# Expert rows picked straight from x, the norm's factor moved into the pick matrix, x in a place of its own, and tile 0 routed before tile 1

## The reference, cut to what matters

```python
h = rms_norm(x, norm_mix[l])
...
x = x + merged @ w_out[l]
h2 = rms_norm(x, norm_ffn[l])
x = x + hier_moe(h2, w_router_group[l], b_router_group[l], w_router_expert[l], b_router_expert[l],
                 w_expert_gate[l], w_expert_up[l], w_expert_down[l])
```

## Time and profile before

| | |
|---|---|
| time, median of 3 runs | 701.91 us (701.51 to 702.41) |
| the profiled execution's own time | 701.26 us |
| its span, first to last instruction | 699.1 us |
| PE busy | 615.8 us, 88% |
| DVE busy | 279.8 us, 40% |
| ACT busy | 199.6 us, 29% |
| bytes moved | 247.53 MB, mean 354 GB/s |

### The profile page before, as it was taken

The page is one execution under the profiler, slowest core; times in us unless marked ns, Lnnn a source line. Parts: engine busy times, 40 slices in busy tenths (PEclk is TensorE's granted clock), DMA queues, the critical chain, the costliest instruction groups (busy, mean ns, idle before and its releaser), DMA issues.

```text
span 699.1 us, 11551 instructions
## 1 busy us (share of the span) xinstructions
PE 615.8 (88%) x4690; PEld 373.8 (53%) x4690; DVE 279.8 (40%) x623; ACT 199.6 (29%) x334; POOL 28.5 (4%) x54
## 2 busy tenths in 40 slices
PE   8999999999999998999987788775878857797876
PEld 5887899999999893333332233322323323332333
DVE  6476976985474945333231112211112211120311
ACT  5684455473535433121111111111111111110111
POOL 2612000000000020000000000000000000000000
PEclk9999999999999999999997989999889998887999
DMA  9995347436479799999999999999999999999995
GB/s 314 309 373 185 133 139 221 155 133 229 166 272 420 304 387 398 428 424 426 429 426 427 429 427 427 427 425 427 428 427 429 425 428 427 428 425 429 426 419 211
DMA packets 40388, 247.53 MB, mean 354 GB/s; under 512 B 4456, under 2 KB 6640, under 8 KB 26128
## 3 DMA queue, kind: packets, MB, share of 16 engines
q1 hardware_dynamic: 37872, 245.44, 86.6%
q0 software_dynamic: 912, 1.25, 1.0%
q10 hardware_dynamic: 1552, 0.10, 0.2%
HBM read 245.72 MB, written 1.06 MB: 353 GB/s over the span
## 4 chain that ended last, share of the span: by engine, by line
PE 57%; DMA 40%; DVE 1%; issue 1%; SPq 0%; POOL 0%; POOLq 0%; DVEq 0%
DMA wide<-in_w_expert_up 35%; PE ps L1431 9%; PE ps L1048 6%; PE ps L1049 6%; PE ps L1050 6%; DMA wide<-in_w_expert_down 5%; PE ps L1468 3%; PE ps L1023 3%; PE ps L1025 3%; PE ps L1024 3%; PE ps L1442 2%; PE ps L1524 2%; PE ps L1079 2%; PE ps L1395 1%; PE ps L1404 1%; PE ps L1091 1%
## 5 line engine op out<-in xcount | busy, mean ns | idle before, releaser
L1431 PE MATMUL ps<-wide,xe 128*32 128x512 f32 x1024 | 147.5, 700 | 72.0 <-DMA wide<-in_w_expert_up 70.2
L2083 DVE TENSOR_TENSOR he<-g_s,ps 128x128 f32<-128x128 f32 x32 | 9.2, 289 | 267.1 <-ACT g_s L935 264.2
L1431 PEld LDWEIGHTS ps<-wide,xe 128*32 128x32 f32 x1024 | 31.2, 119 | 145.0 <-issue 128.8
L1603 DVE TENSOR_TENSOR ring_lo<-ring,w_hi 128x1024 fp32r<-128x1024 f32 x76 | 91.3, 1222 | 41.4 <-ACT w_hi L742 41.0
L742 ACT ACTIVATE w_hi<-ring 128x1024 fp32r<-128x1024 f32 x76 | 78.9, 1057 | 54.8 <-PE ps L1050 34.9
L935 ACT ACTIVATE g_s<-ps 128x128 f32<-128x128 f32 x32 | 8.9, 277 | 252.1 <-PE ps L1442 252.1
L1048 PE MATMUL ps<-hT_hi,w_hi 128*128 128x256 f32 x288 | 80.4, 279 | 0.0
L1049 PE MATMUL ps<-hT_lo,w_hi 128*128 128x256 f32 x288 | 79.5, 276 | 0.0
L1050 PE MATMUL ps<-hT_hi,ring_lo 128*128 128x256 f32 x288 | 79.5, 276 | 0.0
L1524 PE MATMUL ps<-y,back 64*128 64x512 f32 x240 | 59.6, 611 | 1.9 <-ACT y L943 0.9
L1468 PE MATMUL ps<-wide,he 128*32 128x512 f32 x472 | 56.8, 598 | 0.0
(11 more groups left out here) (288 smaller groups left out, 790.9 us busy)
## 6 DMA issues: line engine op xcount, KB each, us to landing
wide<-in_w_expert_gate SPq DMA_DIRECT2D x27, 2048.0 KB, 46.8
wide<-in_w_expert_up SPq DMA_DIRECT2D x27, 2048.0 KB, 48.9
wide<-in_w_expert_down SPq DMA_DIRECT2D x26, 2048.0 KB, 42.5
ring<-in_w_in SPq DMA_DIRECT2D x8, 2048.0 KB, 14.7
ring<-in_w_merge_gate SPq DMA_DIRECT2D x6, 2048.0 KB, 8.7
wide<-in_w_expert_gate SPq DMA_DIRECT2D x10, 1024.0 KB, 9.4
wide<-in_w_expert_up SPq DMA_DIRECT2D x10, 1024.0 KB, 13.5
wide<-in_w_expert_down SPq DMA_DIRECT2D x10, 1024.0 KB, 10.1
```

The source lines that it names most:

```text
L1431: ins = t_.matmul(ps[q * WIN:(q + 1) * WIN, b, :], xe[b][:, j % 2, 2 * c + j // 2, :], w[:, C * j:C * (j + 1)], start=(c == 0 and j < 2), ...
L1603: v.tensor_tensor(piece(ring_lo, g, c), piece(ring, g, c), by_row(out_hi[g == 19][c]).bitcast(F32), ALU.subtract).then_inc(wpre_lo, 1)
```

## The change

1. `pick_rows` multiplies `pick_w` by `x_tok` itself. Its moving operand is now a view of x with a step of 8 floats, 2 rows of 128, in place of 256 floats in a row. Both copies (POOL's and ACT's) and their semaphores go.
2. The norm's factor goes into `pick_w`: for expert 0 by one more small multiplication of `stat` on DVE, for every other expert by a new step `join`, after which `one_row` multiplies by the factor.
3. `x_tok` moves to where nothing is loaded over it, and is also where the final sums are put (`fin`). Place 20 of the ring lies over small tiles of the dense part that are no longer needed. Load 20 stands behind load 16 and waits only for DVE's sums of squares of the first halves.
4. On PE, tile 0's last transposes and its last `route` stand earlier; the last quarter's low-part matmuls get a function of their own, at the place where they were. On DVE, tile 0's `in_group` and `best_two` stand before `x1_add(1, 2)`. The making of `eh` stands behind the first `pick_w`.
5. PE, ACT and DVE read the number of passes ahead of expert 8 (`COUNT_AT`).

```diff
         w_hi = [place(f"w_hi{c}", [P, CW], F32R) for c in range(CHUNKS)]
-        x_at = top[0]
+        top[0] += 192
+        scr_at = top[0]
+        scr = place("scr", [P, 2, C], F32)
+        w_al_at = top[0]
...
+        xn = place("xn_merged", [P, TT, D], F32)
         x_tok = place("x_tok", [P, TT, D], F32)
...
-        fin = [place(f"fin{tt}", [P, D], F32, at=at) for tt, at in enumerate(xn2_at)]
+        fin = [x_tok[:, tt, :] for tt in range(TT)]
...
+                elif n == 20:
+                    sp.wait_ge(halves_squared, 1)
                 else:
-                    sp.wait_ge(seeded, 1)
-                    sp.wait_ge(xn0_ready, 1)
-                    sp.wait_ge(xn1_ready, 1)
...
-            for n in [0, 1, 2, 3, 11] + list(range(4, 11)) + [12, 14, 13, 15, 16, 18, 17, 19, 21, EXTRA, 20]:
+            for n in [0, 1, 2, 3, 11] + list(range(4, 11)) + [12, 14, 13, 15, 16, 20, 18, 17, 19, 21, EXTRA]:
                 first_load(n)
...
-            pool.wait_ge(rstd_ready, 1)
-            g.tensor_scalar(xn2[0][:, :].rearrange("p (k f) -> p k f", k=KD), x_tok[:, 0, :].rearrange("p (f k) -> p k f", k=KD),
-                            stat[:, 40:41], None, ALU.mult).then_inc(xn0_ready, 1)
...
-            act.wait_ge(proj_done, first_bank[NPRE - 2] + 6)
-            act.wait_ge(rstd_ready, 2)
-            s_.activation(xn2[1][:, :].rearrange("p (k f) -> p k f", k=KD), x_tok[:, 1, :].rearrange("p (f k) -> p k f", k=KD),
-                          ACT.Copy, scale=stat[:, 41:42]).then_inc(xn1_ready, 1)
...
-            out_quarter(1, 1, range(0, 2))
+            out_quarter_low(1, 1)
+            turn_x1(0, range(6, KD), 5)
             turn_x1(1, range(4, 6), 4)
-            turn_x1(0, range(6, KD), 5)
-            out_quarter(1, 1, range(2, 5))
-            route(0, range(6, KD), 5)
-            out_quarter(1, 1, range(5, KD))
-            route(1, range(4, 6), 4)
+            out_quarter(1, 1, range(0, 3))
+            route(0, range(6, KD), 4)
+            out_quarter(1, 1, range(3, KD))
+            route(1, range(4, 6), 5)
...
-                        ins = t_.matmul(ps[q * WIN:(q + 1) * WIN, e % 2, 0:QW], pick_w[e % 2][:, tt, :], xn2[tt][:, QW * q:QW * (q + 1)],
+                        rows_q = x_tok[:, tt, :].rearrange("p (f k) -> p k f", k=KD)[:, 2 * q:2 * q + 2, :]
+                        ins = t_.matmul(bank(e % 2, 4)[q * WIN:(q + 1) * WIN, 0:2, :], pick_w[e % 2][:, tt, :], rows_q,
                                         start=(tt == 0), stop=(tt == TT - 1))
...
-                pe.wait_ge(route_ready, 1)
-                pe.reg_load(passes, npass[0:1, 0:1])
                 for e in range(1, NE - 1):
+                    if e == COUNT_AT:
+                        pe.wait_ge(route_ready, 1)
+                        pe.reg_load(passes, npass[0:1, 0:1])
...
             group_of(0)
+            in_group(0)
+            best_two(0)
             x1_add(1, 2)
             square_sum(1, 2)
             mean_square(1)
-            in_group(0)
             scale_out(1)
-            best_two(0)
             group_of(1)
...
+            link(v.tensor_tensor(stat[:, 44:46], stat[:, 44:46], stat[:, 40:42], ALU.mult))
...
+            def join():
+
+                return v.tensor_tensor(same[:, :, 0, :], same[:, :, 0, :], same[:, :, 1, :], ALU.add)
+
             def one_row(dst):
 
-                return v.tensor_tensor(dst[:, :, :], same[:, :, 0, :], same[:, :, 1, :], ALU.add)
+                return v.tensor_tensor(dst[:, :, :], same[:, :, 0, :], rstd, ALU.mult)
...
+                join().then_inc(joined, 1)
+                dve.wait_ge(joined, i + (e + 1))
                 one_row(pick_w[e % 2]).then_inc(chosen_ready, 1)
```

More of the change, by code:

```diff
@@ L81 @@
 EXTRA = 22
+COUNT_AT = 8
 UNITS = 6 * NE
@@ L258, in hybrid_block @@
         probT = aqk[:, 1, :, :].rearrange("p a b -> p (a b)")[:, 0:768].rearrange("p (a b) -> p a b", a=2)
-        xn2_at = (scr_at, w_al_at)
-        xn2 = [place(f"xn2_{tt}", [P, D], F32, at=at) for tt, at in enumerate(xn2_at)]
-        fin = [place(f"fin{tt}", [P, D], F32, at=at) for tt, at in enumerate(xn2_at)]
-        junk = [xn2[0], place("junk", [P, C], F32, at=w_al_at)]
+        fin = [x_tok[:, tt, :] for tt in range(TT)]
+        squares = [place("squares_half", [P, C], F32, at=scr_at)]
+        squares += [place("squares_quarter", [P, QW], F32, at=late_at)] * 2
         here_at = [h2T_at]
@@ L276, in hybrid_block @@
         w_slot = here("w_slot", [P, 2], F32)
-        fold = here("fold", [P, 2, WIN], F32)
+        fold = place("fold", [P, 2, WIN], F32, at=vectors_at)
         tab = place("tab", [P, 2, NE], F32, at=w_r_at)
@@ L1268, in out_half, with low_row, out_begin, out_quarter_low @@
                     ins.then_inc(chunk_done, 1)
-            def out_quarter(tt, q, ks=range(KD)):
-                r = first_bank[19] + tt
-                if ks[0] == 0:
-                    if q == 0:
-                        pe.wait_ge(evacuated[r % 4], r // 4)
-                    else:
-                        pe.wait_ge(x1_ready, tt + 1)
+            def low_row(q, k):
+                return ring_lo[19 % PRE_RING][:, UNIT * q + QW * k:UNIT * q + QW * (k + 1)]
+            def out_begin(tt, q):
+                r = first_bank[19] + tt
+                if q == 0:
+                    pe.wait_ge(evacuated[r % 4], r // 4)
+                else:
+                    pe.wait_ge(x1_ready, tt + 1)
+            def out_quarter_low(tt, q):
+                out_begin(tt, q)
+                for k in range(KD):
+                    ins = t_.matmul(bank(2 * q + tt)[:, 0:QW], merged_hi[:, k, tt * P:(tt + 1) * P], low_row(q, k),
+                                    start=(k == 0), stop=False)
+                ins.then_inc(chunk_done, 1)
+            def out_quarter(tt, q, ks=range(KD)):
+                if tt == 0 and ks[0] == 0:
+                    out_begin(tt, q)
                 rows = slice(tt * P, (tt + 1) * P)
                 o = bank(2 * q + tt)[:, 0:QW]
-                wl = [ring_lo[19 % PRE_RING][:, UNIT * q + QW * k:UNIT * q + QW * (k + 1)] for k in range(KD)]
-                if tt and ks[0] == 0:
-                    for k in range(KD):
-                        ins = t_.matmul(o, merged_hi[:, k, rows], wl[k], start=(k == 0), stop=False)
-                    ins.then_inc(chunk_done, 1)
                 for k in ks:
@@ L1893, in square_sum @@
                 at = 32 + 3 * tt + part
-                link(v.tensor_tensor_reduce(junk[tt][:, 0:cols_p.stop - cols_p.start], x_tok[:, tt, cols_p], x_tok[:, tt, cols_p],
+                link(v.tensor_tensor_reduce(squares[part][:, 0:cols_p.stop - cols_p.start], x_tok[:, tt, cols_p], x_tok[:, tt, cols_p],
                                             1.0, 0.0, ALU.mult, ALU.add, stat[:, at:at + 1]))
@@ L2048, in _ @@
                 link(find(e))
+                link(join())
                 if e == 2:
```

61 lines of the change are left out of this document (31 added, 30 removed).

## The result

The changed kernel takes 703.83 us (median of 7 runs, 703.42 to 705.13), the kernel before 701.68 beside it (7 runs, 700.95 to 702.41). The ratio is 1.0036, 95% interval 1.0024 to 1.0048: slower by 2.15 us by the medians, 2.5 by the ratio. The prediction was 702.1 and no measurable difference. 703.83 lies just inside the upper end of its range, 703.9, but that is luck: that end adds up a dear stepped read and a late landing of the gate weights of expert 4, and the delay that the kernel has ahead of both is in none of its terms. The profiled execution of the changed kernel took 705.13 us, the longest of the seven; its span is 703.0.

A forecast was written before the change was run, and what follows sets the result against it. Experts go at the DMA engines' pace, so the landing of expert 4's gate weights decides: 269.6 + 7.7 + 1.3 = 278.6 against 278.4, +0.2 us on the 701.91 median gives 702.1 us; range 700.0 to 703.9.

The forecast's parts named there:

- upper end of its range: Whole kernel: stepped read at ACT's ratio and 9.6 us landing give 703.4; with run spread, 703.9.
- load 16 landed at 247.33 + 8.7: Load queue before the experts: issue at 247.33 plus 8.7 us puts load 16's landing at 256.0, taken from the kernel before.
- my rivals: Load 20 wins, chance 0.18; stepped read bites, 0.15; load 20 not earlier, 0.05.
- the 270.5 at which the prediction calls itself wrong: Issue of expert 4's gate weights, expected near 269.6; wrong if before 268.5 or after 270.5.
- Load 20: Load queue around routing: loads through it complete 1.4 us earlier, but the hole only moves in front of expert 4's gate weights.
- that no queue explains: Expert 4's gate weights landed 6.2 us behind load 20 where 2 MB need 4.9; the 1.3 us was kept.
- The rival that has load 20 win: Idle time at 254 to 260 us filled, gate weights land as onto an idle queue: 700.0 or 700.4; chance 0.18.
- Rows read with a step: First pick on PE (`pick_rows`): +0.4 us from PE's weight load; bounds nothing and +1.1 us at ACT's ratio.
- the deep case of this rival: Every pick: four quarters run one after the other, 4.3 us a pick, PE becomes the bound, about 726; chance 0.03.
- Tile 0 ahead: Routing on PE and DVE: `x1_add(1, 2)` starts 0.49 us later, putting the path back by 0.37 us.
- The copies, the factor, `join`, the pass count: Routing and experts: no gain from copies, factor free, 0.225 us per pick for `join` hidden, pass count covered at expert 8.
- The sum for the gate weights: Expert 4's gate weights: issue 0.37 + 0.4 = 0.8 us later, at 269.6; landing 278.6 against 278.4, +0.2 us.

The follow-up runs named there:

- e1: Kernel before with only scr placed ahead of x, so the working region lies 4352 bytes higher: 704.55 us, 1.0031.
- e7: Kernel before with scr in front but without the 192 bytes ahead of it, region 4096 bytes higher: 704.55 us, 1.0045.
- e9: Kernel before with scr in front, region 4352 bytes higher, and yc_hi over conv_u instead of scr: 704.92 us, 1.0045.
- e12: Changed kernel with three extra identity transposes on PE ahead of the first branch (155 us): 701.95 us, 1.0006.
- f3: Changed kernel with three transposes ahead of the first branch, and load 20 asked for only behind the first seeds, as late as before: 703.68 us, 1.0030.
- e4: Changed kernel with load 20 back behind the extra place's load, waiting for the seeds as before: 706.30 us, 1.0067.
- f1: Changed kernel with three transposes ahead of the first branch, and the pick reading x in a row (features in another order): 700.70 us, 0.9990.
- f2: Changed kernel with three transposes ahead of the first branch, and DVE's order of before (tile 1's sums ahead of tile 0's choice): 701.68 us, 1.0005.
- e13: Changed kernel with three transposes ahead of each of the seven stretches from the first branch to the third: 704.47 us, 1.0039.

## Why the prediction was wrong, point by point

**The step that failed** is "load 16 landed at 247.33 + 8.7": I took that moment over from the kernel before into the changed one, as if the change did nothing ahead of the routing. I had read that most buffers move and gave their places no price. Load 16 went out at 250.20. The wide spacing that came with the new places cost about 3.0 us of dense part (e1, e7 and e9, with only places changed: 1.0031 to 1.0045; e12 gets it back without moving a buffer), and none of my rivals was of that kind. So the gate weights of expert 4 were issued at 272.93, past the 270.5 at which the prediction calls itself wrong. With the narrow spacing restored (e12) the change comes out at 1.0006, where the forecast was 702.1 / 701.91 = 1.0003. But that agreement is partly luck, since it hides two terms that I had mis-sized against each other:

**Load 20.** Issue and refilled holes came as said (421 and 420 GB/s), and the hole moved in front of the gate weights. That it therefore gains nothing was wrong: 1.7 us in f3, 2.2 in e4. I had carried over 1.3 us between load 20 and the landing of the gate weights "that no queue explains". That term belongs to a late load 20. In the nine profiles that have one the gate weights land 9.0 to 10.1 us behind their issue (9.6 and 9.0 in two profiles of the kernel before), in the eleven others 7.9 to 8.1, where I had added up 9.0. In the changed kernel they landed 30.7 us behind the issue of load 16, before 31.1. The rival that has load 20 win gave 1.5 to 1.9 us.

**Rows read with a step.** I took +0.4 us for the first pick, from PE's weight load. It was +0.95, near ACT's ratio, the upper bound. The single matmul of the pick takes 639 ns, and 379 in f1 with its data in a row; the groups of four quarters start 0.46 us apart instead of 0.22, 2.1 times. The changed kernel, and then f1 (ns min/median/max):

```profile
L1401 PE MATMUL ps<-x_tok,pick_w x512: 619/639/646, 267.1 to 662.8; 128*32 128x256 f32 x171
```

```profile
L1406 PE MATMUL ps<-x_tok,pick_w x512: 376/379/404, 263.7 to 659.0; 128*32 128x256 f32 x171
```

The rule of the Trainium skill ("Advanced Engine Details and Errata", SBUF Cachelines), a penalty where each read hits a new line, holds here with that size; the four quarters still overlap, so the deep case of this rival didn't come.

**Tile 0 ahead.** Counted from load 16, `x1_add(1, 2)` came 0.44 us later than before (predicted 0.49), tile 1's logits 0.32 and the first pick 0.27 (predicted 0.37). Worth nothing measurable (f2).

**The copies, the factor, `join`, the pass count.** No run takes one of them back alone, so that they gain nothing is not shown by itself; e12's +0.4 us less the two measured terms, +1.1 and -1.7, leaves 1.0 us, 0.3 of it for the break, and the intervals are as wide as that. PE's stall of 1.68 us ahead of expert 1 became 1.02, now for `fold`, which DVE makes behind expert 1's `rows_in`. In the experts PE still waits 53.2 us for up weights, so there is time left in which `join` can hide.

**The sum for the gate weights.** Issue predicted 0.8 us later; counted from load 16 it was 22.73 - 21.49 = 1.24 later, 0.95 + 0.27 with a rounding. That everything hangs on the landing of these weights, G, holds: G lies between 276.6 us (f1) and 282.6 (e4) over the 20 profiles, and each kernel's median less its G between 422.8 and 424.6.

**What stays open:** what at a break picks the one spacing or the other; and how the 3.0 us of the profile divide in the median, where the changed kernel loses 2.15 us and others with the same dense part 2.6 to 4.0.

## What to carry to other kernels

A change that moves buffers changes more than their users: count the matmuls per stretch in both traces, far ahead of the edit, before reading the part that was edited. A rhythm of PE that is a few ns wide can be a state and not a price; one cheap break (three transposes, about 0.3 us: six more of them put load 16 back by 1.85 us in e13) tells which, and may buy back 3 us or lose them, so it has to be tried at its place. Two terms that cancel look like a correct forecast: take them back one at a time.

## What the runs showed of the hardware

- A row of equal matmuls of 256 columns, each with new weights, runs at 113.3 or at 117.8 ns from start to start, both at the granted clock of 1.00, for hundreds of matmuls and through changes of operands. Both kernels show both: the one before 117.8 from 11 to 21 us and 113.3 from 155 us on, the changed one the other way round.
- A moving operand read in steps of 32 bytes takes PE 639 ns a matmul instead of 379 in groups of four quarters, and 0.46 us from group to group instead of 0.22 (the changed kernel and f1), 2.1 times, where ACT took 2.03 times as long and PE's weight load 1.36 times.
